# The sum of squares of the first norm: seven chained additions, or pair sums and TensorE adding them up

## The reference, cut to what matters

```python
def rmsnorm(x, g):
    xf = x.astype(jnp.float32)
    y = xf * lax.rsqrt(jnp.mean(xf * xf, axis=-1, keepdims=True) + NORM_EPS)
    return (y * g.astype(jnp.float32)).astype(x.dtype)

h = rmsnorm(x, norm_mix_g[i])
proj = h @ w_in[i].astype(dt)
```

## Time and profile before

| | us |
|---|---|
| median of 3 timed runs | 2630.97 (2630.8 to 2634.1) |
| profiled execution, its time | 2629.82 |
| its span (first to last instruction) | 2628.5 |
| PE busy in it | 2581.3 (98%) |
| DVE busy | 1431.9 (54%) |
| ACT busy | 957.3 (36%) |
| mean granted TensorE clock | 0.997 |

### The profile page before, as it was taken

One profiled execution on the slowest core, in us unless ns is written; L12 is line 12 of the kernel. 1 busy time (PEld: TensorE's weight loads), 2 busy tenths in 40 slices (PEclk: granted clock), 3 DMA queues, 4 the chain that ended last, 5 costly groups with the idle time before them and its releaser, 6 DMA issues.

```text
span 2628.5 us, 35295 instructions
## 1 busy us (share of the span) xinstructions
PE 2581.3 (98%) x14949; PEld 2174.6 (83%) x14949; DVE 1431.9 (54%) x2228; ACT 957.3 (36%) x1803; POOL 157.0 (6%) x178
## 2 busy tenths in 40 slices
PE   8999999999999999999999998999999999999998
PEld 6888888898889788888888977888888888888887
DVE  6785534444565366665664276576633644543434
ACT  5442223453345442323532376332222423322222
POOL 0012110000010010000022000100000100000001
PEclk9999999999999999999999999999999999999999
DMA  3211012222334144562222100265522222222221
GB/s 141 80 65 34 21 42 75 92 70 75 112 112 161 48 177 173 179 224 96 99 77 90 49 1 17 97 234 214 176 96 85 92 96 96 96 96 96 96 93 68
DMA packets 39230, 265.81 MB, mean 101 GB/s; under 512 B 4256, under 2 KB 4512, under 8 KB 8864
## 3 DMA queue, kind: packets, MB, share of 16 engines
q1 hardware_dynamic: 30064, 206.71, 22.6%
q0 software_dynamic: 8320, 55.61, 6.0%
q10 hardware_dynamic: 688, 1.22, 0.1%
HBM read 261.43 MB, written 2.10 MB: 100 GB/s over the span
## 4 chain that ended last, share of the span: by engine, by line
PE 93%; DVE 4%; ACT 3%; issue 0%; DMA 0%; SPq 0%; DVEq 0%; ACTq 0%
PE bank L142 92%; PE bank L145 1%; ACT da_p L148 1%; DVE w_lo L151 1%; DVE da_stat L162 1%; DVE heads_t L159 0%; DVE dd L151 0%; ACT w_hi L148 0%; DMA x_t<-in_x_t 0%; DVE x_t L159 0%; ACT da_pt L148 0%; ACT L148 0%; ACT tmp L148 0%; DVE change L159 0%; DVE tmp L159 0%
## 5 line engine op out<-in xcount | busy, mean ns | idle before, releaser
L142 PE MATMUL bank<-h_hi,w_hi 128*128 128x512 f32 (+1 forms) x1992 | 765.8, 397 | 1.6 <-ACT h_hi L148 1.4
L142 PE MATMUL bank<-h_lo,w_hi 128*128 128x512 f32 (+1 forms) x1992 | 742.7, 391 | 0.0
L142 PE MATMUL bank<-h_hi,w_lo 128*128 128x512 f32 (+1 forms) x1992 | 629.0, 391 | 0.0
L151 DVE TENSOR_TENSOR w_lo<-w_raw,w_hi 128x512 fp32r<-128x512 f32 (+3 forms) x746 | 499.4, 726 | 185.3 <-ACT w_hi L148 184.7
L148 ACT ACTIVATE w_hi<-w_raw 128x512 fp32r<-128x512 f32 (+3 forms) x746 | 424.1, 636 | 294.6 <-PE bank L142 285.1
L142 PEld LDWEIGHTS bank<-h_hi,w_hi 128*128 128x128 f32 (+1 forms) x1992 | 374.1, 188 | 81.8 <-issue 4.9
L142 PEld LDWEIGHTS bank<-h_lo,w_hi 128*128 128x128 f32 (+1 forms) x1992 | 374.1, 188 | 79.5 <-issue 0.8
L142 PEld LDWEIGHTS bank<-h_hi,w_lo 128*128 128x128 f32 (+1 forms) x1992 | 373.0, 188 | 75.7 <-issue 0.4
L142 PE MATMUL bank<-f_hi,w_hi 128*128 128x512 f32 x672 | 262.1, 390 | 0.0
L142 PE MATMUL bank<-f_lo,w_hi 128*128 128x512 f32 x672 | 247.9, 389 | 0.0
L142 PE MATMUL bank<-f_hi,w_lo 128*128 128x512 f32 x672 | 225.9, 389 | 0.0
(11 more groups left out here) (342 smaller groups left out, 3216.3 us busy)
## 6 DMA issues: line engine op xcount, KB each, us to landing
w_raw<-in_pack_ffn SPq DMA_DIRECT2D x60, 1024.0 KB, 4.9
ada_w<-in_ada_w POOLq DMA_DIRECT2D x48, 1024.0 KB, 5.4
w_raw<-in_pack_mlp SPq DMA_DIRECT2D x32, 1024.0 KB, 5.1
w_raw<-in_pack_gdn_qkv SPq DMA_DIRECT2D x12, 1024.0 KB, 4.9
w_raw<-in_pack_sc_cu SPq DMA_DIRECT2D x8, 1024.0 KB, 5.0
w_raw<-in_pack_ffn SPq DMA_DIRECT2D x8, 768.0 KB, 4.2
w_raw<-in_pack_gdn_z SPq DMA_DIRECT2D x4, 1024.0 KB, 5.0
w_raw<-in_pack_gate_a SPq DMA_DIRECT2D x4, 1024.0 KB, 5.0
```

The source lines that it names most:

```text
L142: return self.engine.matmul(*a, **k) if self.engine is not None else self
L151: return self.engine.tensor_tensor(*a) if self.engine is not None else self
```

## The change

The one-column root now stands first in ACT's program, ahead of the squares, and reads a column of `x_t` with scale 0. Tiles 0 to 6 are squared into seven rooms of their own, `rstd`, `sq[0]`, `sq[1]` and the four `tmp` tiles; tile 7 goes into `sq[0]` again once DVE has read it. DVE adds three pairs: 0 and 1, 2 and 3, 4 and 5. PE no longer does three warm-ups ahead; it takes four banks, one for each token chunk, and for each pair sum, and then for tiles 6 and 7 alone, does the four 1-column matmuls, accumulating in the banks. Behind the first and the second of these groups it does one warm-up. ACT's root then reads one column of each of the four banks. Inverse, spread, the two warm-ups behind and all that follows are unchanged. `over_partitions`, `square`, `add_vector` and `root` are no longer used for this norm, but for the others.

```diff
+    MIX_ROOMS, MIX_PAIRS = [rstd, *sq, *tmp, sq[0]], 3
+
+    def mix_sums_tensor(T_, rings):
+        sums = []
+        for c in range(NCH):
+            bank, before = rings.gemm.take(("mix_sums", c))
+            T_.wait_ge(*freed(before))
+            sums.append(bank[:, 0:1])
+        T_.wait_ge(*loaded("consts_loaded"))
+        for i, k in enumerate((0, 2, 4, 6, 7)):
+            T_.wait_ge(*(at("dve_sum", ("mix", k)) if i < MIX_PAIRS else at("act_square", ("mix", k))))
+            for c in range(NCH):
+                done = T_.matmul(sums[c], MIX_ROOMS[k][:, c * P:(c + 1) * P], const("ones")[:, 0:1], start=(k == 0),
+                                 stop=(k == DT - 1))
+            done.then_inc(*up("pe_stat", ("mix", k)))
+            if i < 2:
+                warm_up(T_, rings, ("sums", i), 1)
+
+    def mix_root_scalar(S):
+        S.wait_ge(*at("pe_stat", ("mix", DT - 1)))
+        sums = psum[:, 0:NCH * 512].rearrange("p (c f) -> p c f", c=NCH)[:, :, 0:1]
+        S.activation(stat_cols.rearrange("p (c f) -> p c f", c=NCH), sums, ACT.Sqrt, bias=param("eps"),
+                     scale=1.0 / D).then_inc(*up("act_root", "mix"))
+        for c in range(NCH):
+            counts.let_go["mix_sums", c] = "act_root", counts.n["act_root"]
+
     def in_norm_scalar(S):
+        S.wait_ge(*loaded("x_loaded0"))
+        S.activation(spare_col, x_t[:, 0, 0:1], ACT.Sqrt, scale=0.0)
         for k in range(DT):
-            mix_sum.square(S, k)
+            S.wait_ge(*loaded(f"x_loaded{k // 2}"))
+            if k == DT - 1:
+                S.wait_ge(*at("dve_sum", ("mix", 0)))
+            S.activation(MIX_ROOMS[k][:, :], x_t[:, k, :], ACT.Square).then_inc(*up("act_square", ("mix", k)))
         split_hi(S, 0)
         constants_there(S)
-        mix_sum.root(S)
+        mix_root_scalar(S)
         split_hi(S, 1)
         drain(mix_norm.steps_scalar(S))
 
     def in_norm_vector(V):
-        for k in range(DT):
-            mix_sum.add_vector(V, k)
+        for k in range(0, 2 * MIX_PAIRS, 2):
+            V.wait_ge(*at("act_square", ("mix", k + 1)))
+            V.tensor_tensor(MIX_ROOMS[k][:, :], MIX_ROOMS[k][:, :], MIX_ROOMS[k + 1][:, :], ALU.add).then_inc(
+                *up("dve_sum", ("mix", k)))
         split_lo(V, 0)
         constants_there(V)
         mix_sum.inverse(V)
...
     def tensor_program(T_):
         rings = Rings()
         Ring.holder.clear()
-        warm_up(T_, rings, "sums", 3)
-        mix_sum.over_partitions(T_, rings)
+        mix_sums_tensor(T_, rings)
         mix_sum.spread(T_, rings)
         warm_up(T_, rings, "first", 2)
```

## The result

| | median of runs, us | lowest to highest | sums end in the profile | gates' rows leave PE's bank |
|---|---|---|---|---|
| before | 2632.39 (15 runs) | 2630.80 to 2634.33 | 14.09 | 31.34 |
| after | 2637.75 (15 runs) | 2635.08 to 2639.13 | 19.05 | 37.23 |

The ratio is 1.0021, with a 95% interval of 1.0014 to 1.0028: the change costs 5.4 us. The profiled execution of after took 2638.68 us with a span of 2637.4. That of before, at 2629.82, was shorter than any of its 15 runs, and their median is 1.4 us higher than the one of 3 runs that the prediction started from.

The account below looks back on a forecast made before the run. It took PE, holding 93% of the chain, to bound the kernel. Sums +2.0 and gates +0.4 made +2.4 us on the profiled 2629.82, giving 2632.2; with 1.15 to the median, 2633.4; range 2630.3 to 2637.3.

Parts of the forecast that it names:

- I take a rise between the warm-ups' ends, at 12.5: PE's sums in the first norm: clock goes from 1.2 to 2.4 GHz at 12.5 us, so the tail ends at 16.05.
- Against 14.09: +2.0: End of PE's sums in the first norm: 16.05 us instead of 14.09, a loss of 2.0 us.
- rival B: PE's sums: clock does not rise before the last group, sums end at 19.2, 5.8 us slower, median 2636.8; chance 0.27.
- the stretch at 1629.9: Earlier trace, 1629.9 to 1633.1 us: 1.58 us of 128-column records, else 1-column ones, granted 1.00 and its engine went on so.
- the stretch from 1069.9: Earlier trace, 1069.9 to 1073.3 us: read as nothing but 1-column sums, with the next stretch granted 0.50.
- The spread, which I put at no change: PE's spread behind the first norm's sums: half at each clock level as before, 0.2 either way.
- Gates 0.4: Gates' matmuls behind the first norm: the clock may come back later, costing 0.4 us, bounds 0 to 1.
- No table load and no gain from it: ACT in the first norm: no table load between 3.6 and 36 us; the removed 1.28 us load lay off the path, worth 0.
- Last square near 11.45: ACT in the first norm: the last square is done at 11.45 us instead of 12.06.
- third addition near 11.1: DVE in the first norm: three additions instead of seven, the third finishing at 11.15 us.
- Rival C: PE's sums: a 1-column group takes 0.89 us at either clock level, tail 15.15, +1.05 us, median 2632.0; chance 0.13.
- D: PE's sums: full clock from their start or little behind, ending at 13.97, a gain of 0.1 us, 2630.9; chance 0.10.

Follow-up runs that it names:

- e4: Changed kernel plus a DVE-cleared tile that PE multiplies in four 512-column fp32 matmuls from about 1.5 us, ahead of the sums; 2632.68 us, ratio to before 0.9999.
- e2: Changed kernel without the two warm-ups between the groups of sums, so none ahead of or among them; median 2635.73 us.
- e12: Changed kernel with two warm-ups instead of one behind each of the first two groups of sums, run a second time; median 2639.86 us.
- e3: Kernel before with only the root's table loaded ahead of the squares and the later one-column root gone; 2632.49 us, ratio to before 0.9998.
- e9: Changed kernel with four early 512-column matmuls, a warm-up between sums and spread, and tiles 6 and 7 added on DVE; 2632.41 us, ratio 1.0001.
- e5: Changed kernel with ones stationary and 512 columns of squares moving, no warm-ups between groups, no spread, three warm-ups behind; 2636.98 us, ratio to before 1.0012.

## Why the prediction was wrong

The forecast was 2633.4 us, 2.4 above before and no measurable change; it came out at 2637.75, 5.4 us slower and 0.45 above the range.

**The step that failed** is the one where I chose when the clock rises: "I take a rise between the warm-ups' ends, at 12.5". In the profile it didn't rise before the sums' end at all. The term "Against 14.09: +2.0" measured 4.96. The support I named, that in before it rose between 7.86 and 13.04 "with warm-ups", was of three warm-ups in a row, and not of one between two groups. The row I held against rival B, the stretch at 1629.9 that kept its clock, was about keeping a high clock, and I used it for raising a low one. In e4 a high clock lasted over just these groups and thin warm-ups, to 13.83, and in after, e2 and e12 a low one did not rise with them: the two questions had different answers. I also read the earlier trace rows too simply: the stretch from 1069.9 is not of 1-column sums alone, since from 1072.81 on two of its 30 records have 512 columns. The spread, which I put at no change, took 0.44 more.

**Rival B held, term by term.** Sums' end 19.2 worked out, 19.05 measured. Spread 0.3 longer worked out, 0.44 measured (2.07 against 1.63). Gates 0.4 worked out; measured, the scaling comes 5.49 later (21.99 against 16.50) and the gates' rows 5.89, so 0.4. The sum was 5.8, the start measured 5.89, the median 5.4. B had a chance of 0.27.

**Right as well.** No table load and no gain from it (e3). Last square near 11.45 (11.16, with x 0.3 earlier), third addition near 11.1 (10.84). At full clock the groups end no earlier than before's chain: 13.97 worked out, 13.83 in e4. PE was late by itself, without a gap. The start's shift passed on to the gates' rows and grew there by 0.9, from 4.96 to 5.89.

**Rival C fell.** Weight loads do follow the clock: 333 ns against 192, and a 1-column group 1.71 against 0.89. The Trainium skill, "TensorE: Matmul & The Clock Gate", LDWEIGHTS, gives a length by columns alone, and the measurement decides against reading it as holding at either level. **D** came about only in e4, where matmuls ahead of x had raised the clock.

**The base** was mis-sized too: the median of three runs, 2630.97, stood 1.4 below that of fifteen. Against 2632.39 the same sum for B would have given 2638.2, and the range would have reached 2638.7 and held the 2637.75. So that the time fell outside the range is owed to the base, and that 2.4 us were forecast where 5.4 came is owed to the clock. The highest of the three, 2634.1, was a hint at bunches which I took for spread.

## What to carry to other kernels

Before dropping warm-ups, or putting thin matmuls where dense ones stood, price the new PE work at 1.2 GHz, and take a clock's rise only where a row shows it rise under work like that: rows on how a high clock is kept did not tell it here. A chain moved to PE costs its length in weight loads, 0.89 us for each group of four 1-column fp32 matmuls at full clock and 1.71 at half. At full clock the number of groups behind the last tile is what counts, as e9 shows; at half clock, as in after, all of them and what stands between them. A microsecond at the start is worth measuring in the profile of the start, since stretches at low clock elsewhere move single executions by more.

## What the runs showed of the hardware that I had not expected

- A reciprocal of 128x512 fp32 on DVE took 3.35 us, where an addition of the same shape takes 0.69 and a reciprocal of 128x4 0.18.
- The clock rose under sums with 512 moving columns, 1.7 us each at the lower level, without any warm-up (e5); under sums of the same data with one moving column it did not, in 8.7 us (e2). One profile of each shows it.
- The stretches view gives a granted clock of 1.00 for the start of after, where the weight loads of the sums took 333 ns (median of each group of records): at this start only durations tell the level.
- The same instructions behind the start took 2597.1 to 2601.4 us from profile to profile, by how often and how long PE fell to 1.2 GHz.
